# Four samples in rows 0 to 31 and four in rows 32 to 63: the state product of a gated delta layer, split by rows

## The chip, the cores and the metric

The kernel runs on one core of a Trainium2 chip. The metric is device time in microseconds (us) of one execution, the median of several runs.

## What is computed

One step of a hybrid decoder layer, in float32, over 512 prompt tokens and 8 samples of 8 tokens each. What the change touches is the gated delta rule of the sample tokens, with 8 heads of 128 x 128. Cut to that:

```python
def step(s, c):                       # a block of tokens of one sequence and head
    vw_c, kd_c, qk_c, qd_c, ko_c, gl_c = c
    u = vw_c - jnp.einsum('bhcd,bhde->bhce', kd_c, s)
    o = jnp.einsum('bhcd,bhde->bhce', qd_c, s) + jnp.einsum('bhij,bhje->bhie', qk_c, u)
    s = gl_c[..., None, None] * s + jnp.einsum('bhcd,bhce->bhde', ko_c, u)
    return s, o
```

For the samples, b runs over 8 sequences and c over 8 tokens, and `s` is returned as `new_delta_sample`. Per head and sample, the last product of `step` contracts 8 tokens: keys (8 x 128) times `u` (8 x 128) give the 128 x 128 update of the state.

## The kernel before

Channels lie on partitions, tokens along the free axis: 576 columns, 512 of the prompt and 64 of the samples. There are two big parts. The first is the mixing part, a loop of phases n = 0 to 8, written out by hand as 32 slots s for each engine. In phase n TensorE streams the input projection of the next head (the function `dense`, line 558: passes of 288 columns, three for each product, since weights and activations are split in a high and a low part), and between those pieces the delta rule of head n - 1 is worked on, head 1 in phase 1 up to head 8 in phase 8. Phases 2 to 7 are a hardware loop. Below, "head n" is phase n. The second part, from 716 us on, is the output projection (line 567) and the feed-forward part (lines 529 and 883), nearly all TensorE.

The sample state lies in `v["ss"]`, 128 partitions by 8 samples x 128 columns. Its update in phase n has these steps, in the order in which they depend on each other:

- Slot 26: ScalarE writes `u` of the samples, 64 rows (8 samples x 8 tokens) by 128 columns. GpSimd then copies it 8 times side by side into `v["um"]` (64 x 1024), times the mask `rowm`, so that block q keeps only the rows of sample q. It posts `um_ready`.
- Slot 29: GpSimd multiplies `v["ss"]` by its decay and posts `ss_decayed`. It waits for `o_ps`, TensorE's last product for the prompt.
- Slot 30, line 778: TensorE multiplies the keys (`v["ko"]`, 64 rows by 128 columns) with `v["um"]`, in two products of 512 columns into PSUM banks 4 and 5, and posts `ss_ps`. A float32 product is two passes for TensorE, each with its own load of weights.
- Slot 30: VectorE (`sample_state`, line 1338 in the profile) adds the two banks to `v["ss"]` and posts `ss_ready`; two taps of a convolution (line 1341) follow on its queue.
- Slot 31: TensorE sums squares (line 577), ScalarE takes a logarithm and an exponential of the sums (lines 1190 and 1192), and VectorE scales the head's output into `o_a` and posts `head_out`.
- Slot 0 of the next phase: ScalarE (line 1125) waits for `head_out`, and normalizes keys and queries; the chain of the next head runs from there. In its slot 7 TensorE transposes at line 684.

In phase 8 the state isn't added in slot 30: VectorE does it later, in the output part. There GpSimd multiplies blocks of `conf` by a gate (`gate_b`) behind its masked copy, and VectorE adds those blocks to `o_a`.

Every engine has its own queue, which is worked off in order, with waits on counting semaphores.

Of the kernel before, what the change touches and what calls it, by code (L numbers as in the profile page):

```python
# [31 lines left out]
P = 128  # L32
# [3 lines left out]
SEQ = 512  # L36
NS, LS = 8, 8
SMP = NS * LS
# [18 lines left out]
LEVELS_S = 3  # L57
# [22 lines left out]

_LAYOUT = [("ident", P), ("ones", P), ("tri", P), ("suf", P), ("tri_s", SMP), ("suf_s", SMP),
           ("eps", 1), ("eps128", 1), ("big", P), ("big_s", SMP), ("lvl", LEVELS * P),
           ("lvl_s", LEVELS_S * SMP), ("strict", P), ("rowm", NS)]
OFF, _o = {}, 0
for _n, _w in _LAYOUT:
    OFF[_n] = (_o, _o + _w)
# [9 lines left out]
def build(nc, x_t, w_all, w_log, log_par, consts, params, taps, halos, s_in,  # L96
          y_out, s_prompt, s_sample, qkv_rows, conf_rows):
    with ExitStack() as ctx:
# [22 lines left out]
        at, v = 0, {}  # L121
# [46 lines left out]
        def con(nm, rows=P):  # L168
            a, b = OFF[nm]
            return cst[0:rows, a:b] if b <= WIDE else masks[0:rows, a - WIDE:b - WIDE]  # L170
# [13 lines left out]
        def job_ps(j2):  # L184
            return ps[:, 2 * j2:2 * j2 + 2, 0:HALF]

        def g(i):
            return ps[:, 4 + i, :]
# [4 lines left out]
        def two(ap):  # L193
            return ap.rearrange("p (a b) -> p a b", a=2)
# [4 lines left out]
        def tile(ap, c):  # L199
            return ap[:, c * P:c * P + P]  # L200

        def sm(ap, rows=SMP):
            return ap[0:rows, SEQ:SEQ + SMP]

        def smw(ap):
            return ap[0:SMP, SEQ:SEQ + P]
# [176 lines left out]
        def xc_squares(k):  # L383
            nm = ("c4", "extq", "extk", "extv", "qc", "kc", "vc", "gext")[k]
            return v[nm][:, 0:TOK]
# [126 lines left out]
        def _(pe):  # L512
            mm = nc.tensor.matmul
# [60 lines left out]
            def ones_sum(dst, src, start=True, stop=True):  # L574

                for h in range(2):
                    r = mm(dst[:, h], con("ones"), src[:, h * HALF:(h + 1) * HALF],  # L577
                           start=start, stop=stop)
                return r
# [44 lines left out]
            def phase(n):  # L624
                gdn, proj = not first(n), not last(n)
                segs = 0
                for s in range(32):
# [59 lines left out]
                    if s in range(8, 21, 2):  # L687
# [7 lines left out]
                        for c in range(TILES):  # L695
                            r = mm(tile(g(0), c), tile(w, c), tile(t, c),  # L696
                                   start=True, stop=True)
                        if l <= LEVELS_S:
                            r = mm(g(2)[0:SMP, 0:SMP], c_s[(l - 1) % 2][0:SMP], sm(v["dm"]), start=True, stop=True)
                        r.then_inc(x_ps, 1)  # L700
                    if s in range(9, 22, 2):
# [7 lines left out]
                        if l <= LEVELS:  # L709
                            for c in range(TILES):  # L710
                                r = mm(tile(g(0), c), tile(u_r, c), tile(x_r, c), start=True, stop=True)  # L711
                            if l < LEVELS_S:
                                r = mm(g(2)[0:SMP, 0:SMP], v["us"][0:SMP], sm(v["db"]), start=True, stop=True)
                            r.then_inc(dt_ps, 1)
                        for c in range(TILES):
                            r = mm(tile(g(1), c), tile(x_r, c), tile(u_r, c), start=True, stop=True)  # L716
                        if l <= LEVELS_S:
                            r = mm(g(3)[0:SMP, 0:SMP], sm(v["db"]), v["us"][0:SMP], start=True, stop=True)
# [20 lines left out]
                    if s in (22, 24, 26, 28):  # L739

                        c = (s - 22) // 2
                        if c:
                            pe.wait_ge(s_ready, TILES * n - 4 + c)
                        r = mm(g(1)[:, 0:P], tile(u_all, c), tile(v["vt"], c), start=True,  # L744
                               stop=c == 0)
                        if c:
                            r = mm(g(1)[:, 0:P], tile(v["kn"], c), v["s"], start=False, stop=True)
# [3 lines left out]
                    if s in (23, 25, 27, 29):  # L751

                        c = (s - 23) // 2
# [6 lines left out]
                        r = mm(tile(g(3), c), tile(v["u"], c), tile(v["qk"], c), start=c == 0, stop=True)  # L760
                        if c == TILES - 1:
                            r.then_inc(o_ps, 1)
                    if s == 23:
# [5 lines left out]
                        for q in range(NS):  # L769
                            r = mm(two(g(2)[:, 0:2 * SMP])[:, :, q * LS:(q + 1) * LS], tile(v["ss"], q),  # L770
                                   kq[:, :, SEQ + q * LS:SEQ + (q + 1) * LS], start=q == 0, stop=q == NS - 1,
                                   skip_group_check=True)
                        r.then_inc(sz_ps, 1)
                    if s == 30:
                        pe.wait_ge(um_ready, n)
                        pe.wait_ge(s_ready, TILES * n)
                        for q in range(2):
                            r = mm(g(q), smw(v["ko"]), v["um"][0:SMP, q * SEQ:(q + 1) * SEQ],  # L778
                                   start=True, stop=True)
                        r.then_inc(ss_ps, 1)  # L780
                    if s == (30 if last(n) else 31):
# [7 lines left out]
                    if last(n) and s == 20:  # L789

                        pe.wait_ge(xc_ready, KB)
                        for k in range(0, KB, 2):
                            pe.wait_ge(xc_pair, k // 2 + 1)
                            r = ones_sum(job_ps(1), xc_squares(k), k == 0, k == KB - 2)
                        r.then_inc(var_ps, 1)

            phase(0)
            phase(1)
            with pe.Fori(2, H) as n:
                phase(n)  # L800
# [1007 lines left out]
        def _(pool):  # L1808
            gp = nc.gpsimd

            def tt(out, a, b, op):
                return gp.tensor_tensor(out, a, b, op)  # L1812
# [39 lines left out]
            def phase(n):  # L1852
# [8 lines left out]
                for s in range(33):  # L1861
# [97 lines left out]
                        tt(pr(v["um"]), pr(t_r.bitcast(F32)), bc(con("ident")), ALU.subtract).then_inc(tmi_ready, 1)  # L1959
                    if s == 26:  # L1960
                        pool.wait_ge(us_ready, n)
                        tt(v["um"][0:SMP, :].rearrange("p (q c) -> p q c", q=NS),
                           smw(v["u"]).unsqueeze(1).to_broadcast([SMP, NS, P]),
                           con("rowm", SMP).unsqueeze(2).to_broadcast([SMP, NS, P]),
                           ALU.mult).then_inc(um_ready, 1)
                    if s == 29 and not last(n):

# [9 lines left out]
                    if last(n) and s == 31:  # L1977
                        gate_b(7, 0)

            phase(0)  # L1980
            phase(1)
            with pool.Fori(2, H) as n:
                phase(n)
# [45 lines left out]
def shape_constants():  # L2029

    i, j = np.indices((P, P))
    a, b = np.indices((SMP, SMP))
    same = a // LS == b // LS
    out = np.zeros((P, CONSTS), np.float32)

    def put(nm, value, at=0):
        o = OFF[nm][0] + at
        out[:value.shape[0], o:o + value.shape[1]] = value

    def half(r, c, n):  # L2040
        return (r // (2 * n) == c // (2 * n)) & (r // n < c // n)

    put("ident", i == j)
    put("ones", np.ones((P, P)))
    put("tri", i <= j)
    put("suf", i > j)
    put("big", np.where(j < i, BIG, 0))
    put("tri_s", same & (a <= b))
    put("suf_s", same & (a > b))
    put("big_s", np.where(same & (b >= a), 0, BIG))  # L2050
    for l in range(LEVELS):
        put("lvl", half(i, j, 2 ** l), l * P)
    for l in range(LEVELS_S):
        put("lvl_s", half(a, b, 2 ** l), l * SMP)
    put("strict", i < j)
    put("rowm", np.arange(SMP)[:, None] // LS == np.arange(NS)[None, :])
    put("eps", np.full((P, 1), EPS))
    put("eps128", np.full((P, 1), P * EPS))
    return out
# [84 lines left out]
```

## Time and profile before

| | us |
|---|---|
| median of 3 runs | 1191.23 |
| lowest and highest run | 1190.07, 1191.61 |
| the profiled execution | 1191.59 |
| its span, first to last instruction | 1189.5 |

| engine | busy us | share of the span |
|---|---|---|
| TensorE, multiplies | 1148.7 | 97% |
| TensorE, weight loads | 1096.0 | 92% |
| VectorE | 726.2 | 61% |
| GpSimd | 610.2 | 51% |
| ScalarE | 518.5 | 44% |

In the profile's rows PE is TensorE, PEld its weight loads, DVE VectorE, ACT ScalarE, POOL GpSimd and SP SyncE. A row names the line of the kernel, what it writes `<-` what it reads, and the shape; most tiles of the delta rule are parts of one tensor, `work`, and all are called so. The multiplies of TensorE overlap, so that their durations add up to more than the time they take: the distance between two starts is what one costs. GpSimd's tensor operations all have line 1812, VectorE's 1338 or 1341, since a helper issues them; shapes tell them apart.

### The profile page before, as it was taken

To read this page: it belongs to the slowest core of one execution; us is meant where nothing else is said; L and a number is where in the kernel's file an instruction comes from. 1 tells how busy PE (TensorE), PEld (TensorE's weight loads), DVE (VectorE), ACT (ScalarE), POOL (GpSimd) and SP (SyncE) were. 2 spreads that over 40 slices of the span, in tenths; PEclk is the share of its full clock that TensorE was granted. 3 is DMA by queue.
4 is the path that set the end of the run, shared out by engine and by line. 5 is a ranking of instruction groups with operands and counts; after the bars stand their busy time and mean duration, and the time that the engine had idled before them with its cause. 6 is when DMAs were issued, how large, how long until landed. Compare 5 with 4: busy or idle time off the path is not lost.

```text
span 1189.5 us, 22147 instructions
## 1 busy us (share of the span) xinstructions
PE 1148.7 (97%) x8349; PEld 1096.0 (92%) x8349; DVE 726.2 (61%) x1064; ACT 518.5 (44%) x898; POOL 610.2 (51%) x480
## 2 busy tenths in 40 slices
PE   6789999999999999999999989999999999999996
PEld 5689989899899998999989979999999999999996
DVE  6678896886868868778683546764135215314735
ACT  6554545544445354553462576542133123213531
POOL 0338558386584764847657374332433433435841
PEclk9899999999999999999999999999999999999998
DMA  6211223112222122121321116212222222222212
GB/s 236 61 57 45 75 73 100 57 35 81 74 72 83 31 85 74 50 78 44 98 93 41 49 38 222 71 54 72 77 83 90 73 87 88 71 88 89 91 35 80
DMA packets 32519, 92.28 MB, mean 78 GB/s; under 512 B 4688, under 2 KB 12240, under 8 KB 32464
## 3 DMA queue, kind: packets, MB, share of 16 engines
q1 hardware_dynamic: 32464, 91.52, 23.7%
q8 instruction: 38, 0.62, 0.2%
q14 instruction: 17, 0.14, 0.0%
HBM read 82.99 MB, written 8.52 MB: 77 GB/s over the span
## 4 chain that ended last, share of the span: by engine, by line
PE 77%; DVE 11%; issue 6%; ACT 4%; POOL 1%; DMA 0%; DVEq 0%; SPq 0%; ACTq 0%; POOLq 0%
PE ps L529 29%; PE ps L558 23%; PE ps L567 6%; DVE work L1338 5%; PE ps L883 4%; DVE ps L1341 4%; PE ps L716 2%; PE ps L696 2%; PE ps L711 2%; PE ps L770 1%; PE ps L778 1%; PE ps L744 1%; PE ps L577 1%; PE ps L590 1%; DVE o_a L1341 1%
## 5 line engine op out<-in xcount | busy, mean ns | idle before, releaser
L1812 POOL TENSOR_TENSOR w_lo<-raw,w_hi 128x1024 fp32r<-128x1024 f32 x123 | 298.6, 2429 | 380.3 <-ACT w_hi L981 225.8
L558 PE MATMUL ps<-in_hi,w_hi 128*128 128x288 f32 x992 | 305.7, 308 | 3.0 <-ACT work L1058 2.8
L558 PE MATMUL ps<-in_hi,w_lo 128*128 128x288 f32 x992 | 300.3, 303 | 0.0
L558 PE MATMUL ps<-in_lo,w_hi 128*128 128x288 f32 x992 | 299.0, 301 | 0.0
L558 PEld LDWEIGHTS ps<-in_hi,w_hi 128*128 128x128 f32 x992 | 188.9, 190 | 6.6 <-ACT w_hi L963 3.0
L558 PEld LDWEIGHTS ps<-in_hi,w_lo 128*128 128x128 f32 x992 | 188.9, 190 | 2.0
L558 PEld LDWEIGHTS ps<-in_lo,w_hi 128*128 128x128 f32 x992 | 188.8, 190 | 1.2
L1341 DVE SCALAR_TENSOR_TENSOR ps<-work,ct,ps 128x512 f32<-128x512 f32 x240 | 180.7, 753 | 7.4 <-DVE work L1460 1.7
L981 ACT CAST w_hi<-raw 128x1024 fp32r<-128x1024 f32 x61 | 63.8, 1047 | 224.3 <-PE ps L529 224.3
L1338 DVE TENSOR_TENSOR f_tmp<-f_tmp 128x576 f32<-128x576 f32 x31 | 70.7, 2282 | 96.4 <-ACT f_tmp L1288 91.0
L1338 DVE TENSOR_TENSOR o_a<-o_a,ps 128x576 f32<-128x576 f32 (+1 forms) x40 | 25.3, 634 | 144.7 <-PE ps L529 122.8
L529 PE MATMUL ps<-in_hi,w_hi 128*128 128x288 f32 x464 | 99.4, 296 | 0.1
L529 PE MATMUL ps<-in_hi,w_lo 128*128 128x288 f32 x464 | 99.4, 296 | 0.0
L529 PE MATMUL ps<-in_lo,w_hi 128*128 128x288 f32 x464 | 99.3, 296 | 0.0
L963 ACT CAST w_hi<-raw 128x1024 fp32r<-128x1024 f32 x64 | 66.9, 1045 | 36.1 <-PE ps L558 35.1
L529 PE MATMUL ps<-f_lo,w_hi 128*128 128x288 f32 x384 | 82.6, 296 | 0.0
L529 PE MATMUL ps<-f_hi,w_hi 128*128 128x288 f32 x384 | 82.5, 296 | 0.0
L529 PE MATMUL ps<-f_hi,w_lo 128*128 128x288 f32 x384 | 82.5, 296 | 0.0
L1145 ACT ACTIVATE x_r<-ps 128x512 fp32r<-128x512 f32 x48 | 28.8, 599 | 110.7 <-PE ps L696 57.0
L529 PEld LDWEIGHTS ps<-in_hi,w_hi 128*128 128x128 f32 x464 | 74.7, 189 | 0.3 <-issue 0.3
L529 PEld LDWEIGHTS ps<-in_hi,w_lo 128*128 128x128 f32 x464 | 74.8, 189 | 0.0
L529 PEld LDWEIGHTS ps<-in_lo,w_hi 128*128 128x128 f32 x464 | 74.8, 189 | 0.0
(290 smaller groups left out, 2396.0 us busy)
## 6 DMA issues: line engine op xcount, KB each, us to landing
raw<-w_all_in SPq DMA_DIRECT2D x136, 512.0 KB, 3.6
work<-s_in_in SPq DMA_DIRECT2D x8, 512.0 KB, 3.6
s_sample_out<-work SPq DMA_DIRECT2D x8, 512.0 KB, 2.7
xt<-x_t_in SPq DMA_DIRECT2D x4, 576.0 KB, 6.4
xt<-x_t_in SPq DMA_DIRECT2D x2, 1152.0 KB, 7.5
y_out<-o_a SPq DMA_DIRECT2D x16, 144.0 KB, 1.7
halo<-halos_in SPq DMA_DIRECT2D x9, 156.0 KB, 3.4
conf_rows_out<-c_rows SPq DMA_DIRECT2D x8, 135.0 KB, 2.2
```

The lines of the kernel that those rows point to most:

```text
L529: r = mm(ps[:, 2 * w + h, 0:HALF], a[:, k], b[:, k, h * HALF:(h + 1) * HALF], start=k == 0 and p3 == 0, stop=k == KB - 1 and p3 == 2)
L558: t = mm(dense_ps(n, j, h), a[:, w, k], b[:, k, h * HALF:(h + 1) * HALF], start=r == 0, stop=r == PASS_MM // 2 - 1)
L567: r = mm(dst, a[:, k], half_of(b[:, k], h), start=k == 0 and p3 == 0, stop=k == KB - 1 and p3 == 2)
L696: r = mm(tile(g(0), c), tile(w, c), tile(t, c), start=True, stop=True)
L711: r = mm(tile(g(0), c), tile(u_r, c), tile(x_r, c), start=True, stop=True)
L883: r = mm(half_ps(i % 4), a[:, k], half_of(b[:, k], h), start=k == 0 and p3 == 0, stop=k == KB - 1 and p3 == 2)
L963: nc.scalar.copy(w_hi[:, w_buf(n, j)], raw[:, raw_slot(n, j)]).then_inc(w_high, 1)
L981: nc.scalar.copy(weight(m, off)[0], raw[:, (off + 2) % RING]).then_inc(w_high, 1)
L1145: r = A(x_r[:], g(0), ACT.Copy)
L1338: return ve.tensor_tensor(out, a, b, op)
L1341: return ve.scalar_tensor_tensor(out=out, in0=a, scalar=s_, in1=b, op0=op0, op1=op1)
L1812: return gp.tensor_tensor(out, a, b, op)
```

## The change

The keys and the masked `u` contract over 32 rows in each of the two products in place of 64. Product q takes rows 32q to 32q + 31 of both, that is samples 4q to 4q + 3. The masked copy has 4 blocks of 128 columns in place of 8: in rows 0 to 31 block c is sample c, in rows 32 to 63 it is sample 4 + c. The mask has 4 columns. Both products read the same 512 columns of `v["um"]`, from different rows. Results, banks, semaphores, waits and the order on every engine stay as they are.

```diff
@@ -80,7 +80,7 @@
-           ("lvl_s", LEVELS_S * SMP), ("strict", P), ("rowm", NS)]
+           ("lvl_s", LEVELS_S * SMP), ("strict", P), ("rowm", NS // 2)]
@@ -775,7 +775,8 @@
                         for q in range(2):
-                            r = mm(g(q), smw(v["ko"]), v["um"][0:SMP, q * SEQ:(q + 1) * SEQ],
+                            rows = slice(q * SMP // 2, (q + 1) * SMP // 2)
+                            r = mm(g(q), v["ko"][rows, SEQ:SEQ + P], v["um"][rows, 0:SEQ],
                                    start=True, stop=True)
                         r.then_inc(ss_ps, 1)
@@ -1959,9 +1960,9 @@
                         pool.wait_ge(us_ready, n)
-                        tt(v["um"][0:SMP, :].rearrange("p (q c) -> p q c", q=NS),
-                           smw(v["u"]).unsqueeze(1).to_broadcast([SMP, NS, P]),
-                           con("rowm", SMP).unsqueeze(2).to_broadcast([SMP, NS, P]),
+                        tt(v["um"][0:SMP, 0:SEQ].rearrange("p (q c) -> p q c", q=NS // 2),
+                           smw(v["u"]).unsqueeze(1).to_broadcast([SMP, NS // 2, P]),
+                           con("rowm", SMP).unsqueeze(2).to_broadcast([SMP, NS // 2, P]),
                            ALU.mult).then_inc(um_ready, 1)
@@ -2053,7 +2054,7 @@
-    put("rowm", np.arange(SMP)[:, None] // LS == np.arange(NS)[None, :])
+    put("rowm", np.arange(SMP)[:, None] // LS % (NS // 2) == np.arange(NS // 2)[None, :])
```

## Rows read from the trace of the kernel before

**Rows 1.** The page, busy us of each engine (share of the span) and instructions.
```profile
PE 1148.7 (97%) x8349; PEld 1096.0 (92%) x8349; DVE 726.2 (61%) x1064; ACT 518.5 (44%) x898; POOL 610.2 (51%) x480
```
**Rows 2.** The page, shares of the span in the chain that ended last.
```profile
PE ps L529 29%; PE ps L558 23%; PE ps L567 6%; DVE work L1338 5%; PE ps L883 4%; DVE ps L1341 4%; PE ps L716 2%; PE ps L696 2%; PE ps L711 2%; PE ps L770 1%; PE ps L778 1%; PE ps L744 1%; PE ps L577 1%; PE ps L590 1%; DVE o_a L1341 1%
```
**Rows 3.** A stretch: its length, then busy PE, PEld, DVE, ACT, POOL, clock, DMA.
```profile
474.00:550.00 76.00, 75.57 (x552) 70.25 (x552) 58.85 (x94) 36.43 (x72) 48.41 (x48) 1.00 0.21 67
```
**Rows 4.** Line 778: ns min/median/max, first and last start; who waited (us, times).
```profile
L778 PE MATMUL ps<-work x32: 589/589/693, 145.0 to 709.1; 64*128 64x512 f32 x32
...
  DVE work L1338: 9.2, 6
```
**Rows 5.** The chain that ended last, around head 6: start us, us, what.
```profile
526.84 1.92 PE ps L778 x4
...
532.35 0.83 DVE o_a L1341
...
551.77 0.66 PE ps L684 x4
```
**Rows 6.** Timeline of line 778 in head 6: start us, us, engine, line [idle before].
```profile
526.76 0.29 PEld L778 LDWEIGHTS ps<-work 64*128 64x128 f32 x2 [0.17 <-issue]
526.77 0.69 PE L778 MATMUL ps<-work 64*128 64x512 f32 x1
...
527.73 1.02 PE L778 MATMUL ps<-work 64*128 64x512 f32 x2
...
528.16 0.59 PE L778 MATMUL ps<-work 64*128 64x512 f32 x1
```
**Rows 7.** Timeline of head 6, the engines around line 778.
```profile
520.58 1.89 POOL L1812 TENSOR_TENSOR work<-work,masks 64x1024 f32<-64x1024 f32 x1 [0.74 <-ACT work L1172]
...
525.71 3.27 POOL L1812 TENSOR_TENSOR work<-work 128x1024 f32<-128x1024 f32 x2 [3.24 <-PE ps L760]
...
528.78 1.22 DVE L1338 TENSOR_TENSOR work<-work,ps 128x1024 f32<-128x1024 f32 x1 [1.53 <-PE ps L778]
...
529.95 0.74 ACT L1190 ACTIVATE work<-ps,cst 128x576 f32<-128x576 f32 x1 [0.67 <-PE ps L577]
...
531.56 0.76 DVE L1338 TENSOR_TENSOR work<-o_a,work 128x576 f32<-128x576 f32 x1
```
**Rows 8.** TensorE's waits from 474 to 550 us: us in total, times, longest.
```profile
PE ps L684 <- DVE work L1338: 0.4, 1, 0.4
```
**Rows 9.** Timeline of head 1 at line 778.
```profile
144.48 3.12 DVE L1341 SCALAR_TENSOR_TENSOR ps<-work,ct,ps 128x512 f32<-128x512 f32 x4
...
144.99 1.98 PE L778 MATMUL ps<-work 64*128 64x512 f32 x4
...
147.52 1.21 DVE L1338 TENSOR_TENSOR work<-work,ps 128x1024 f32<-128x1024 f32 x1
```
**Rows 10.** GpSimd's groups by shape: count, busy us, mean ns, idle before.
```profile
L1812 POOL TENSOR_TENSOR work<-work,masks 64x1024 f32<-64x1024 f32 x8 | 15.1, 1887 | 5.1 <-ACT work L1172 5.1
...
L1812 POOL TENSOR_TENSOR work<-work 128x1024 f32<-128x1024 f32 x7 | 13.4, 1913 | 22.7 <-PE ps L760 22.7
...
L1812 POOL TENSOR_TENSOR work<-work,masks 128x512 f32<-128x512 f32 x8 | 9.8, 1231 | 0.0
...
L1812 POOL TENSOR_TENSOR work<-cst,hc 128x512 f32<-128x512 f32 x8 | 8.3, 1040 | 43.8 <-DVE hc L1617 43.8
```
**Rows 11.** Timeline of the last head: GpSimd, VectorE, TensorE.
```profile
704.25 7.84 POOL L1812 TENSOR_TENSOR conf<-conf,gate 128x576 f32<-128x576 f32 x5
...
711.35 1.35 DVE L1338 TENSOR_TENSOR conf<-conf,o_a 128x576 f32<-128x576 f32 x1
...
712.63 0.75 DVE L1338 TENSOR_TENSOR conf<-conf,o_a 128x576 f32<-128x576 f32 x1
...
716.32 0.53 PE L567 MATMUL ps<-in_hi,w_more 128*128 128x288 f32 x2 [0.98 <-DVE in_lo L1338]
```
**Rows 12.** The chain that ended last, in the last head.
```profile
706.13 5.82 DVE conf L1338 x4
```

## Prediction, made before the changed kernel ran

> **What bounds the kernel now.** I read the busy shares first. TensorE is busy 97% of the span, VectorE 61%, GpSimd 51% [rows 1], and of a stretch of 76 us, about one head, TensorE is busy 75.57 us [rows 3]. So time taken from TensorE can count, and time taken from GpSimd is suspect until a wait on it is found. The chain that ended last comes next: it gives line 778, the two products that this change rewrites, 1% of the span [rows 2]. The view of that line says why: its 32 passes take 0.59 us each, and VectorE waited 9.2 us for them, six times [rows 4], 1.53 us a time. Six, not eight: heads 2 to 7. In the chain of such a head the four passes (1.92 us) hand over to VectorE, then to `o_a` and ScalarE, and the chain comes back to TensorE only at line 684, 23 us later [rows 5], where TensorE waits 0.4 us [rows 8]. That return is the point to watch: a gain on TensorE alone would become a longer wait at line 684, while a gain that also moves VectorE's step is kept.
>
> **What the change does to TensorE.** There are still two products per head, each 512 columns wide and each in two passes, so 32 passes in all. Nothing shorter is streamed. A pass starts 0.43 us after the one before (527.73 to 528.16) and lasts 0.59 us by its record [rows 6]. What changes is that product 0 uses rows 0 to 31 and product 1 rows 32 to 63, with results in two different PSUM banks. Before, all four passes used rows 0 to 63, one after another. The trace of before shows no pass that starts in a row other than 0, so whether two such passes run side by side has to be bounded. From below: they don't, and four slots stay four (gain 0). From above: product 1 lies wholly beside product 0, and four slots become two (gain 2 x 0.43 = 0.86 us). I take one slot, 0.43 us. TensorE's starts in every timeline stand in program order, and the two passes of a product use the same rows, so the order is 0a, 0b, 1a, 1b: only 0b and 1a are neighbours with different rows. Three slots, then, with the last pass starting at 527.73 and not 528.16.
>
> The Trainium skill, TensorEngine Tiling (Array Packing), Key Properties, says that different tiles can load weights and multiply in parallel, and TensorE: Matmul & The Clock Gate, Part 3, adds that multiplies stay strictly in program order. By these two the gain is the one slot that I took. The same page says that a product over 32 rows alone takes as long as one over 128 rows, so without concurrency it would be nothing. No row here shows concurrency either way.
>
> Where products of 128 rows give way to line 778's of 64, there is a gap of 0.17 us, and the first pass lasts 0.69 us and not 0.59 [rows 6]. That change of shape stays, so it costs nothing new. From row 0 to row 32 the shape stays the same; I take 0 there, with 0.17 + 0.10 = 0.27 us as the other bound.
>
> **Who moves with it, heads 2 to 7.** VectorE's addition starts at 528.78, after a wait of 1.53 us on line 778. It waits also for GpSimd's decay of the states, which starts at 525.71 and takes 1.91 us, to 527.62 [rows 7, 10], and VectorE itself was free at 528.78 - 1.53 = 527.25. So the addition can move forward by up to 1.16 us, and 0.43 fits. ScalarE's logarithm waits 0.67 us for TensorE's sums behind line 778 [rows 7], so it moves 0.43 too, and the next VectorE product at 531.56 needs both. TensorE's own queue is 0.43 us earlier as well. All three arrive at line 684 earlier by the same amount: the wait of 0.4 us stays as it is, and the head is 0.43 us shorter. Six heads: 6 x 0.43 = 2.58 us.
>
> **Head 1: nothing.** There VectorE runs four convolution taps from 144.48 for 3.12 us, to 147.60, and the addition follows at 147.52 without a wait, while TensorE's passes ended at 146.97 [rows 9]. TensorE's 0.43 us turns into a longer wait in the next head.
>
> **What the change does to GpSimd.** The masked copy shrinks from 64x1024 (1.887 us) to 64x512. The nearest rows are the same operation with a mask at 128x512 (1.231 us) and one with a column operand at 128x512 (1.040 us); halving the old one gives 0.94 us [rows 10]. I take 1.2 us, since the operation with a mask has the same kinds of operands: 0.69 us saved, bounds 0.65 and 0.95. In heads 2 to 7 it is worth nothing: the copy starts at 520.58, ends at 522.47, and TensorE comes for it at 526.77 [rows 6, 7]; a cover of 4.3 us.
>
> **The last head: GpSimd's saving counts.** Behind the copy GpSimd has five multiplications of `conf` without a break, 704.25 to 712.09 [rows 11], and VectorE's additions of the same blocks are the chain from 706.13 [rows 12]. A VectorE addition of 128x576 takes 0.75 us alone but 1.35 us where it still overlaps GpSimd [rows 11]. If GpSimd's run ends 0.69 us earlier, at 711.40, the addition at 711.35 is alone nearly from its start and takes 0.75 to 0.8 us. TensorE waits 0.98 us at 716.32 for what follows from it [rows 11], so 0.5 to 0.6 us comes through: 0.57 us (bounds 0.3 and 0.6). Line 778 itself is not on the chain here.
>
> **The small rest.** The constant `rowm` has 4 columns in place of 8, so a load and a cast at the start carry 4 columns fewer of 1416: under 0.01 us. Order and waits of every engine stay the same.
>
> **Sum.** 2.58 + 0.57 = 3.15 us. The profiled execution took 1191.59 us (span 1189.5), so 1188.44 by its own time. The median of the runs is 0.36 us below the profiled one, so I forecast 1188.1 us, 0.26% faster.
>
> **Rivals.**
>
> *No side by side.* Rows 0 to 31 and rows 32 to 63 take turns, and four slots remain. For it: no row shows two passes of line 778 less than 0.43 us apart. Against it: nothing in the trace could have shown it, since all start at row 0. Then only the last head gains: 1191.23 - 0.57 = 1190.7, no change. If the change of rows also cost a gap of 0.27 us, it would be 6 x 0.27 - 0.57 = +1.05, 1192.3, still no change. Chance 0.24.
>
> *Two slots.* Both products run whole beside each other, 0.86 us a head on TensorE. ScalarE then limits: its logarithm can come only 0.67 us earlier [rows 7]. So 6 x 0.67 + 0.57 = 4.6 us, 1186.6. Against it: pass 0b would have to wait behind nothing, though it uses the same rows as 0a. Chance 0.08.
>
> The Trainium skill, TensorE: Matmul & The Clock Gate, Part 3, gives a measured speedup of 3.07 for four products over 32 rows each. [...]
>
> *Slower: loads exposed.* Today the second pass's weights are loaded while the first runs (two loads from 526.76, done at 527.05). A pass that had to wait for the end of the one before, as the first one does with its 0.69 us, would take 0.69 and not 0.43 us of TensorE's time, 0.26 us more [rows 6]. If smaller row groups lost that hiding, three of the four passes would each cost 0.26 us, 0.78 us a head on the chain, since VectorE already waits there: 6 x 0.78 - 0.57 = +4.1 us, 1195.3. It makes the kernel measurably slower from two such passes a head (6 x 0.52 - 0.57 = +2.6). Against it: the 64-row products already hide their second load. Chance 0.08.
>
> **How the numbers follow.** The forecast has a chance of 0.60, with a range of its own from 1187.3 to 1188.9 (the bounds of the last head, 0.3 us, and half of the 1.54 us over which the runs of before spread). Under 0.2% (2.4 us, so above 1188.85) this kernel's measurement can hardly be told from no change; about 0.52 of the 0.60 lies below that. Faster: 0.52 + 0.08 = 0.60. Same: 0.08 + 0.24 = 0.32. Slower: 0.08. The range reaches to two slots below and to no side by side above: 1186.4 to 1191.0; outside it lie the slower rival and a gap between the rows.
>
> **What the new profile would show.** Right: at the two products the third pass starts within some hundredths of the second, the last about 0.86 us after the first (not 1.29), VectorE's wait for it falls from 1.53 to 1.10 us in six heads, the wait at line 684 stays at 0.4 us, and starts of heads drift apart by 0.43 us a head. GpSimd's copy reads 64x512 at about 1.2 us, and the addition in the last head takes about 0.75 us. Wrong: starts 0.43 us apart as now, or the gain on TensorE found again at line 684. What would break the sum is a VectorE wait that turns from line 778 to GpSimd's decay, or a last head in which VectorE and GpSimd overlap all the same.

## The result, and the profile after

| | us |
|---|---|
| median before, 8 runs | 1191.98 |
| median after, 8 runs | 1185.64 (1184.15 to 1188.24) |
| ratio of the times | 0.9947, 95% interval 0.9934 to 0.9960 |
| profiled execution after, its span | 1188.01, 1185.9 |

The change takes 6.3 us, 0.53%, where 3.15 us were forecast; the time lies below the range. The direction was right, the forecast was half of what came. The range was laid from the median of 1191.23 us, from which the result is 5.6 us away; the median of the eight runs of before is 0.75 us higher. In two more comparisons on other chips the ratio was 0.9945 (0.9932 to 0.9958) and 0.9954 (0.9939 to 0.9968).

The profiled execution happens to be one of the slowest of the eight, so its span is only 3.6 us shorter than that of before. I come back to that at the end of the experiments; the parts of a head can be read from it all the same. First the view of the two products' line (779 after; before in [rows 4]): durations in ns as min/median/max, first and last start, who waited (us in total, times, longest us).

```profile
L779 PE MATMUL ps<-work x32: 587/640/692, 145.3 to 703.7; 32*128 32x512 f32 x32
...
  DVE work L1339: 4.1, 6
```

VectorE still waits six times, but 4.1 us in total and not 9.2. The timeline of head 6 around them, to be laid beside [rows 6] and [rows 7] (start us, us, engine, line, and in brackets the idle time before):

```profile
522.80 3.29 POOL L1813 TENSOR_TENSOR work<-work 128x1024 f32<-128x1024 f32 x2 [4.10 <-PE ps L760]
...
523.85 0.30 PEld L779 LDWEIGHTS ps<-work 32*128 32x128 f32 x4 [0.17 <-issue]
523.86 1.13 PE L779 MATMUL ps<-work 32*128 32x512 f32 x4
...
524.91 1.24 PE L577 MATMUL ps<-work,cst 128*128 128x288 f32 x4
525.03 1.22 DVE L1339 TENSOR_TENSOR work<-work,ps 128x1024 f32<-128x1024 f32 x1 [0.69 <-PE ps L779]
525.68 0.69 ACT L1040 ACTIVATE work<-work 128x576 f32<-128x576 f32 x1
526.27 0.72 ACT L1191 ACTIVATE work<-ps,cst 128x576 f32<-128x576 f32 x1
527.03 0.69 ACT L1193 ACTIVATE work<-work 128x576 f32<-128x576 f32 x1
...
527.86 0.76 DVE L1339 TENSOR_TENSOR work<-o_a,work 128x576 f32<-128x576 f32 x1 [0.15 <-ACT work L1193]
```

All four loads now run within 0.30 us, and all four passes within 1.13 us in place of 1.98. Cut to shorter stretches of the same timeline, the four passes fall into two pairs:

```profile
523.86 0.70 PE L779 MATMUL ps<-work 32*128 32x512 f32 x2
...
524.39 0.59 PE L779 MATMUL ps<-work 32*128 32x512 f32 x2
```

In the records a pair's two starts are 6 to 7 ns apart (523.855 and 523.862, 524.389 and 524.395). Two slots, then, not three. The next products, line 577, start 1.06 us after line 779's first pass (524.912 - 523.855); before it was 1.91 us. TensorE gives 0.85 us in each head.

VectorE's scaling of the head's output, at 527.86, comes 4.00 us after the first pass (before, 531.56 - 526.77 = 4.79, so 0.79 us less), and waits 0.15 us for ScalarE, whose three operations from 525.68 on stand one behind the other without a gap. A head is 75.50 us long: the line starts at 448.36, 523.86 and 599.36, where before it started 76.30 us apart. From head 1 to head 2 it is 76.57 us (before 76.58): head 1 gives nothing. The wait at line 684 (before in [rows 8]) is nearly as it was:

```profile
PE ps L684 <- DVE work L1339: 3.0, 6, 0.5
```

This is of the whole run (us in total, times, longest us); before, the same row was 3.0 us in 7 waits. In head 6 alone it went from 0.42 to 0.48 us, of which more below. GpSimd's copy, 1.89 us in [rows 7], takes 1.03 us:

```profile
517.67 1.03 POOL L1813 TENSOR_TENSOR work<-work,masks 64x512 f32<-64x512 f32 x1 [0.73 <-ACT work L1173]
```

### The profile page after: what moved, and what is told of

It reads as the page before. It is cut to its first block, busy times and chain, and to the rows that moved or that the text cites. A ratio compares the mean times of both kernels' runs of the same rounds, so it can differ in the third digit from the quotient of the medians.

```text
span 1185.9 us, 22147 instructions
## 1 busy us (share of the span) xinstructions
PE 1143.2 (96%) x8349; PEld 1093.7 (92%) x8349; DVE 727.3 (61%) x1064; ACT 517.3 (44%) x898; POOL 602.5 (51%) x480
## 4 chain that ended last, share of the span: by engine, by line
PE 78%; DVE 10%; ACT 5%; issue 5%; POOL 1%; DMA 0%; DVEq 0%; SPq 0%; ACTq 0%; POOLq 0%
PE ps L529 29%; PE ps L558 24%; PE ps L567 6%; PE ps L884 4%; DVE work L1339 4%; DVE ps L1342 3%; PE ps L716 2%; PE ps L696 2%; PE ps L711 2%; PE ps L770 1%; PE ps L744 1%; PE ps L577 1%; DVE conf L1339 1%; DVE o_a L1342 1%; PE ps L590 1%
## 5 line engine op out<-in xcount | busy, mean ns | idle before, releaser
L558 PEld LDWEIGHTS ps<-in_hi,w_lo 128*128 128x128 f32 x992 | 189.5, 191 | 2.1
L1339 DVE TENSOR_TENSOR t_r<-t_r,ps 128x512 fp32r<-128x512 f32 x48 | 33.0, 688 | 68.8 <-PE ps L711 61.6
```

What stands on the lines that cost most here:

```text
L558: t = mm(dense_ps(n, j, h), a[:, w, k], b[:, k, h * HALF:(h + 1) * HALF], start=r == 0, stop=r == PASS_MM // 2 - 1)
L1339: return ve.tensor_tensor(out, a, b, op)
```

## The experiments

The theory after the result (A): what a head gains comes from passes over different rows running side by side, in pairs, and GpSimd's copy counts only in the last head. Against it stood that the copy is worth more (B), that the clock's scatter made the gain (C), and that a product over 32 rows is simply faster (D).

### The whole change again, and each half alone

e1 and e9 are the changed kernel itself. e1 to e4 ran beside the kernel before on one chip, e5 to e8 on a second and e9 to e12 on a third; e5, e6 and e7 were run once each, for their traces.

> The changed kernel once more, beside its two halves on the same chip. Theory A (the saving is the four passes of line 779 taking two slots of 0.43 us and not four, 0.80 us in each of heads 2 to 7): starts of line 779 are 75.50 us apart in heads 2 to 7, against 76.30, four passes within 1.13 us, and the time is 4.8 us or a little more below the kernel before. Rival C (a good part of the measured 6.3 us was scatter of the granted clock between runs): the same head period, with times that spread by 3 us or more and follow the granted clock of each run.

The rows alone (e2, e10); GpSimd's copy stays 64x1024:

```diff
-   r = mm(g(q), smw(v["ko"]), v["um"][0:SMP, q * SEQ:(q + 1) * SEQ],
+   rows = slice(q * SMP // 2, (q + 1) * SMP // 2)
+   r = mm(g(q), v["ko"][rows, SEQ:SEQ + P], v["um"][rows, q * SEQ:(q + 1) * SEQ],
```

> TensorE's half alone: the products use rows 0 to 31 and rows 32 to 63, but GpSimd still writes the full 64x1024 masked copy, and product q reads its columns 512q to 512q + 511. Theory A: head period 75.50 us, as with the whole change, and the time within 1 us of it. Rival B (GpSimd's shorter copy is what counts in the time, by way of the last head): the gain falls by 1.5 us or more against the whole change.

The copy alone (e3, e11), against the changed kernel. Both products read the same 512 columns over all 64 rows, so the samples are not kept apart:

```diff
-   r = mm(g(q), v["ko"][rows, SEQ:SEQ + P], v["um"][rows, 0:SEQ],
+   r = mm(g(q), smw(v["ko"]), v["um"][0:SMP, 0:SEQ],
```

> GpSimd's half alone: the masked copy is 64x512, and both products still contract over 64 rows, each over the same 512 columns, so that samples are mixed in the state sums and the sample states are not those of the reference. Theory A: head period 76.30 us as before, four passes 0.43 us apart, time between the one before and 0.6 us below it. Rival B: 1.5 us or more below the kernel before.

| kernel | median us (before, same chip) | ratio, interval | head period |
|---|---|---|---|
| e1 whole | 1186.05 (1192.31) | 0.9945, 0.9932 to 0.9958 | 75.49 |
| e2 rows | 1188.24 (1192.31) | 0.9960, 0.9946 to 0.9974 | 75.49 |
| e3 copy | 1190.75 (1192.31) | 0.9989, 0.9980 to 0.9997 | 76.30 |
| e9 whole | 1185.84 (1191.52) | 0.9954, 0.9939 to 0.9968 | 75.50 |
| e10 rows | 1188.96 (1191.52) | 0.9972, 0.9962 to 0.9983 | 75.48 |
| e11 copy | 1191.45 (1191.52) | 0.9999, 0.9990 to 1.0008 | 76.30 |

VectorE's wait for the products in e3, by the view of their line (us in total, times); in e2 it is 4.1 us, as in the whole change:

```profile
  DVE work L1338: 9.2, 6
```

The head period is decided by the rows alone, to 0.02 us, and the copy moves no head: on that point B falls. The times do not settle what the copy is worth. Alone it takes 1.3 us by the ratio in e3 (1.6 us between the medians) and 0.1 us in e11. Beside the rows it looks larger: e2 is 1.8 us slower than e1 by the ratios (2.2 us between the medians), where A allowed 1 us and B asked for 1.5 us, and e10 is 2.1 us slower than e9 (3.1 us between the medians), where 0.7 us had been expected. The rows alone gave 4.8 us in e2 and 3.3 us in e10. So by their times the halves of the second comparison add up to 3.4 us, and the whole change took 5.5 us. Like stretches of the traces give the copy 0.7 us, as the last section of the experiments shows; the rest of the difference is not explained. The expectations of the second comparison:

> The changed kernel, on one chip with its two halves and with the early square, to see the sum of its parts in the times. By the sections of the traces so far: 4.84 us from the row split (five periods of 0.80 and 0.82 in the seventh), 0.70 us from the shorter copy: 5.5 us below the kernel before, ratio 0.9954. If the scatter of the granted clock falls differently, between 4.5 and 7 us.

> The row split with the full copy once more: 4.8 us below the kernel before and 0.7 us above the whole change. From head 8's state product to the first product of line 529: 78.4 us, against 77.7 with the shorter copy, where one window of low clock falls between 690 and 705 us in both.

> The shorter copy alone once more (samples mixed in the state sums, as before): 0.7 us below the kernel before; if it is 1.5 us or more again, the copy is worth more than the section of the last head shows.

### Is it the separate rows?

e4: both products over rows 0 to 31, so samples 4 to 7 get the sums of samples 0 to 3.

```diff
-   rows = slice(q * SMP // 2, (q + 1) * SMP // 2)
+   rows = slice(0, SMP // 2)
```

> Both products contract over rows 0 to 31 (samples 4 to 7 get the sums of samples 0 to 3, so the sample states are not those of the reference); all else as in the changed kernel. Theory A (passes on different rows run side by side, those on the same rows take turns): four starts 0.43 us apart, as before the change, and a head period of 76.30 us. Rival D (a product over 32 rows is itself faster, or its two passes go side by side whatever the rows): two slots here too, 1.13 us for the four passes and 75.50 us a head.

e6: product 0 over rows 0 to 63, product 1 over rows 64 to 127, with whatever lies there; the sample states are not the right ones here either.

```diff
-   rows = slice(q * SMP // 2, (q + 1) * SMP // 2)
-   r = mm(g(q), v["ko"][rows, SEQ:SEQ + P], v["um"][rows, 0:SEQ],
+   rows = slice(q * SMP, (q + 1) * SMP)
+   r = mm(g(q), v["ko"][rows, 0:P], v["um"][rows, 0:SEQ],
```

> Row groups of 64 in place of 32: product 0 contracts over rows 0 to 63 and product 1 over rows 64 to 127, taking keys of prompt tokens and what lies in the masked copy's columns there (so the sample states are not those of the reference). Theory A (it is the separate rows that count, not that there are 32): two slots, 1.13 us for four passes, head period 75.50 us. Rival D (only products over 32 rows go side by side): four slots and 76.30 us.

The timeline of head 6 in e4:

```profile
527.04 1.98 PE L779 MATMUL ps<-work 32*128 32x512 f32 x4
```

And the same in e6:

```profile
524.09 1.13 PE L779 MATMUL ps<-work 64*128 64x512 f32 x4
```

Over the same 32 rows the four passes take the 1.98 us of before, the head 76.29 us, and VectorE waits its 9.2 us again; over two separate groups of 64 rows they take 1.13 us and the head 75.50 us. So rival D falls: 32 rows are not faster than 64, and it is the separate rows that pair. The whole time of e4, 1191.24 us (ratio 0.9992, 0.9982 to 1.0002), is again that of before. In all these runs the two products write to two different PSUM banks; in e4 that alone made no pair, and whether passes on separate rows would pair within one bank was not tried.

### How do two products make two slots?

My forecast let only neighbours in program order pair. e5 puts a product in between:

```diff
-   for q in range(2):
+   for q in (0, 0, 1):
```

> The changed kernel with product 0 issued twice: rows 0 to 31, rows 0 to 31 again (the same result once more), rows 32 to 63. It asks how passes find their place. Theory A1 (each group of rows works off its own passes, and one that waits does not hold up another group's): six passes in four slots, those of the last product at 0.01 and 0.53 us beside those of the first, the other four 0.43 us apart. Theory A2 (a product goes beside the one just ahead of it in the program and no further): four slots too, but the last product's passes begin with the second product's, at about 0.96 us. Theory A3 (strictly in order of passes, the step that my forecast rested on): five slots. The head period is 76.3 us in A1 and A2, 76.7 in A3.

The timeline of head 6, in four stretches:

```profile
527.19 0.70 PE L779 MATMUL ps<-work 32*128 32x512 f32 x2
...
527.72 1.02 PE L779 MATMUL ps<-work 32*128 32x512 f32 x3
...
528.15 1.02 PE L779 MATMUL ps<-work 32*128 32x512 f32 x2
```

The six passes start at 527.19 (two, 13 ns apart), 527.72 (two, again 13 ns apart), 528.15 and 528.58: four slots, the pairs first. The head period is 76.29 us, 0.79 us more than with two slots. That is A1. Which record belongs to which product can be told by the signal: only the last product of the program posts it, and the record that carries it is the one that starts at 527.735, second of its pair. So the last product does not wait behind the second, whose rows are busy. Each group of rows works off its own passes in these traces; my order 0a, 0b, 1a, 1b was the order of the program and not of the array. What still comes in order is the end: VectorE's addition, which waits for the last product's signal, started only at 529.22, when the last of all passes ended (528.58 + 0.59 = 529.17):

```profile
529.22 1.22 DVE L1339 TENSOR_TENSOR work<-work,ps 128x1024 f32<-128x1024 f32 x1 [1.55 <-PE ps L779]
```

The Trainium skill, TensorE: Matmul & The Clock Gate, Part 3, says that multiplies keep the program's order in start and end. For the signal this case agrees; for the starts e5 does not, since passes of the product between start 0.95 us (528.151 to 527.202) and 0.85 us after those of the product behind it.

### What holds a head at 0.80 us?

TensorE gave 0.85 us and the head 0.80; what lies between them is the longer wait at line 684. In e7 ScalarE's square of the keys (line 1040) moves from behind the table load to slot 29:

```diff
 if s == 29:
+    if not last(n):
+        square_k(n)
     act.wait_ge(o_ps, n)
@@ slot 31
     log_exp()
-    square_k(n)
```

> The changed kernel with one move on ScalarE: the square of the keys goes from behind the table load at line 954 to slot 29, where ScalarE idles 1.4 us, so that the logarithm of line 1191 is no longer behind it. Theory E (ScalarE's queue is what holds the gain of a head at 0.80 us where TensorE gave 0.86): head period 75.43 to 75.46 us. Rival F (another engine holds it): 75.50 us.

> The version with ScalarE's square of the keys in slot 29, timed: head period 75.44 us, six times 0.06 us and so 0.4 us below the changed kernel, less than the scatter of the runs; the trace's period decides, the time only if it is 1 us or more away.

The period is 75.44 us in both runs of this kernel, so theory E holds: ScalarE's queue took the last 0.06 us. Its logarithm now waits for TensorE again (head 6 of e7):

```profile
525.21 1.28 ACT L954 ACT_TABLE_LOAD   x1
527.01 0.74 ACT L1192 ACTIVATE work<-ps,cst 128x576 f32<-128x576 f32 x1 [0.51 <-PE ps L577]
```

TensorE's wait at line 684 is back at its old length. Head 6 of before, of the first profile after, and of e7:

```profile
551.77 0.66 PE L684 MATMUL ps<-cst,c_r 128*128 128x128 f32 x4 [0.42 <-DVE work L1338]
```

```profile
548.07 0.66 PE L684 MATMUL ps<-cst,c_r 128*128 128x128 f32 x4 [0.48 <-DVE work L1339]
```

```profile
548.83 0.66 PE L684 MATMUL ps<-cst,c_r 128*128 128x128 f32 x4 [0.43 <-DVE work L1340]
```

The median of e12 was 1184.20 us (ratio 0.9948, 0.9931 to 0.9964) beside 1185.84 of e9. It is the lowest median of all versions, but the 1.6 us between the two (0.7 us by the ratios) are inside the intervals; the traces carry 0.3 us of them (453.79 against 454.07 us from head 1's product to head 7's).

e8 went further and put the sums (line 577) ahead of the state products on TensorE, and two of VectorE's convolution taps from slot 30 to slot 29:

```diff
@@ TensorE, slot 30
+    pe.wait_ge(o_sq, n)
+    pe.wait_ge(o_read, 2 * n)
+    ones_sum(g2(2), v["gk"]).then_inc(o_sums, 1)
     (the two state products)
-    the same three lines, slot 31
@@ VectorE
-   late = {..., 28: 2, 29: 2, 30: 2, 31: 2}
+   late = {..., 28: 2, 29: 4, 31: 2}
```

> A further version: the square of the keys early as in the run before, TensorE sums the squares (line 577) ahead of the state products, and VectorE takes the two taps of slot 30 in slot 29. The scaling of the head's output then can start at 0.6 us earlier within the head. Theory E (the chain through VectorE and ScalarE ends last, until TensorE's own 0.4 to 0.5 us of waiting at line 684 is used up): head period 75.0 to 75.1 us, 2.4 to 3.0 us less in six heads. Rival G (TensorE's queue ends last already): 75.4 us or more.

The period is 75.57 us, longer than that of e7 (the time: 1186.92 us, ratio 0.9960, 0.9944 to 0.9975). The chain of head 6 shows why (start us, us, what):

```profile
524.51 1.20 PE ps L558 x9
525.72 0.07 issue
525.78 1.21 PE ps L577 x4
526.99 1.06 PE ps L783 x4
528.05 1.78 PE ps L558 x12
529.83 1.94 PE ps L577 x8
531.77 3.44 PE ps L558 x26
...
539.02 0.38 PE ps L663 x2
...
549.94 0.66 PE ps L684 x4
```

By their starts the sums and the products take 2.20 us of TensorE there (525.78 to 527.98). In the changed kernel the products take 1.06 us to the start of line 577, and the sums 0.86 us more to the next one, 1.92 us. TensorE alone is the chain from 518 to 539 us, as rival G had it; from there to line 684 it is mostly VectorE, as in the changed kernel. So the earlier scaling moved nothing behind 539 us, where VectorE waits for TensorE's line 663. Over one head TensorE is busy 75.24 us and not 75.02, and waits 0.07 us ahead of the sums; the wait at line 684 gives back 0.21 us (0.48 to 0.27), and does not go to nothing as theory E had hoped. e8 makes three moves at once, and which of them cost what was not taken apart.

### The last part of the mixing, and the scatter

The stretch from head 7's state product to the first product of line 529 holds the seventh head's gain, the last head and the output projection. TensorE's granted clock from 630 to 645 us sorts the runs (starts from the timelines):

| kernel | from, to | us | clock, 630 to 645 us |
|---|---|---|---|
| before | 603.05, 786.15 | 183.10 | 0.89 |
| e3 copy | 604.81, 787.19 | 182.38 | 0.89 |
| e2 rows | 601.70, 783.96 | 182.26 | 0.89 |
| e4 same rows (copy alone) | 603.33, 784.21 | 180.88 | 1.00 |
| e10 rows | 600.68, 781.61 | 180.93 | 1.00 |
| e1 whole | 599.26, 779.32 | 180.06 | 1.00 |
| first profile after | 599.36, 782.57 | 183.21 | 0.77 |

The row of that stretch in before (stretch, length, busy PE, PEld, DVE, ACT, POOL, clock, DMA share, GB/s):

```profile
630.00:645.00 15.00, 14.03 (x94) 13.00 (x92) 3.53 (x7) 3.75 (x9) 14.33 (x14) 0.89 0.17 46
```

The same in the first profile after:

```profile
630.00:645.00 15.00, 14.03 (x84) 13.18 (x82) 3.12 (x7) 3.08 (x8) 10.87 (x10) 0.77 0.22 70
```

And in e1:

```profile
630.00:645.00 15.00, 14.03 (x107) 13.27 (x106) 3.52 (x8) 4.84 (x10) 13.04 (x12) 1.00 0.23 72
```

Like against like: at 0.89 the copy takes 0.72 us (183.10 to 182.38) and the rows 0.84 us; at 1.00 the rows take 0.82 us (180.88 to 180.06). The copy's 0.87 us at 1.00 (180.93 to 180.06) is less alike, since from 690 to 705 us e10's clock is 0.77 and e1's 0.89. Between 0.89 and 1.00 with the same kernel work lie 1.50 us (e3 to e4), and between 0.77 and 1.00 3.15 us (first profile to e1). In e6, which has the same passes and copy and a clock of 1.00 in all of 630 to 720 us, the stretch takes 180.25 us, 2.96 less than in the first profile.

What the shorter copy does in the last head shows in e3, to be laid beside [rows 11]:

```profile
705.13 7.33 POOL L1812 TENSOR_TENSOR conf<-conf,gate 128x576 f32<-128x576 f32 x5
...
707.79 6.62 DVE L1338 TENSOR_TENSOR conf<-conf,o_a 128x576 f32<-128x576 f32 x5
```

VectorE's five additions start 1.70 us ahead of the state product (707.75 us before, 709.49 in e3) in both, but GpSimd's run beside them ends 1.37 us earlier against it (2.97 and not 4.34 us after it), and they take 6.62 us in place of 7.33. TensorE's wait of 0.98 us in [rows 11] is 0.32 us in e3.

TensorE's busy time from 630 to 645 us is 14.03 us in all three rows above, with a wait of about 1 us in each, and yet its clock was at the lower of its two levels, 1.2 GHz, for part of the stretch in before, for twice that in the first profile after, and never in e1. The runs of one kernel (the first profile after, and e1) differ in it as much as different kernels do. This is why the spans of the first two profiles differ by 3.6 us where the medians differ by 6.3: in the stretch of the table the first profile after gains nothing. There is a second place of scatter. Up to head 1's product the traces of all kernels take from 144.67 to 148.07 us: 144.99 before, 145.28, 145.23 and 144.67 with the whole change, 147.66 and 146.69 with the rows alone, 146.74 and 147.27 with the copy alone. The change does nearly nothing there, and whether the halves are slower there by chance, two traces of each cannot say; it would go some way towards the times of e2 and e10. Rival C is right on the scatter and wrong on the cause: the periods of heads carry the gain.

e9, not in the table, took 181.73 us at 1.00, 1.48 more than e6: its low clock came from 705 to 720 us (0.89), where the output projection starts. Between, from 690 to 705 us, low clock did not add up in the same way: e1, at 0.89 there, took 0.19 us less than e6. From head 7's product to head 8's it took 102.33 us and not 100.83, and got that back behind it, 77.73 and not 79.42 us. VectorE's additions of `conf` are stretched by GpSimd beside them. The timeline of the last head in the first profile after, whose clock is 1.00 from 690 to 705 us:

```profile
700.36 6.82 POOL L1813 TENSOR_TENSOR conf<-conf,gate 128x576 f32<-128x576 f32 x5
...
701.47 8.33 DVE L1339 TENSOR_TENSOR conf<-conf,o_a 128x576 f32<-128x576 f32 x5
```

And in e1, whose clock is 0.89 from 690 to 705 us:

```profile
697.26 7.34 POOL L1813 TENSOR_TENSOR conf<-conf,gate 128x576 f32<-128x576 f32 x5
...
699.89 6.66 DVE L1339 TENSOR_TENSOR conf<-conf,o_a 128x576 f32<-128x576 f32 x5
```

In the first, VectorE starts 1.1 us behind GpSimd and takes 8.33 us; in the second it starts 2.6 us behind, and takes 6.66. The sums end 2.6 us after GpSimd in one and 1.95 us in the other: what a late start costs VectorE it gets back from the shorter overlap.

## Why the prediction was off, step by step

**What bounds the kernel: right.** Line 778 was on the chain in heads 2 to 7 and VectorE waited for it; a saving that TensorE and VectorE share came through, with the wait at line 684 0.06 us longer.

**The slot: the step that failed.** I bounded the saving by 0 and 0.86 us and took one slot, 0.43, because "the order is 0a, 0b, 1a, 1b: only 0b and 1a are neighbours with different rows". The premise, that starts keep the program's order, was read from a kernel in which every pass started at row 0 and could not have shown anything else. Measured: 0.85 us (1.91 to 1.06), the upper bound but for 0.01, and e5 shows the order broken. VectorE's wait fell from 1.53 to 0.69 us, not to 1.10. The rival "two slots" was the right one, at a chance of 0.08. It should have had far more: nothing in the trace spoke against it but the order that I took from passes on the same rows.

**The cap by ScalarE: right in kind, too low in size.** I let ScalarE move by its 0.67 us of waiting. Its logarithm moved by 0.77 (3.18 to 2.41 us behind the first pass), since an operation's recorded duration is not its place in the queue: line 1040 is recorded with 0.69 us, but the next started 0.59 us later. The scaling behind it moved by 0.79, the head by 0.80. e7 shows the cap itself. With 0.80 the rival would have read 6 x 0.80 + 0.57 = 5.4 us, 1185.9 us; the range's lower end of 1186.4, which hung on the 0.67, would have come to about 1185.6, at the edge of the result.

**Change of shape from row 0 to row 32: 0, right.** The second product starts 7 ns after the first.

**Head 1: nothing, right** (76.58 and 76.57 us to the next head).

**GpSimd's copy: right in kind, a little small, and partly by luck.** 1.03 us and not 1.2, and in heads 2 to 7 worth nothing. The last head: 0.57 us forecast, 0.72 measured between like runs. I had one addition, the fourth, fall from 1.35 to 0.75 us. In e3 it did, to 0.74; but the third fell too, from 1.95 to 1.34, and the first grew from 1.62 to 2.13, beside a GpSimd that was further ahead of VectorE all along. Those two nearly cancel.

**The sum.** Forecast 2.58 + 0.57 = 3.15 us. The traces give, for heads 2 to 6, 458.06 - 454.08 = 4.0 us from head 1's product to head 7's, 0.8 for the seventh and 0.7 for the copy: 5.5 us. The three timed comparisons gave 6.3, 6.6 and 5.5 us (by their ratios), and 5.5 lies in each interval. What remains above it in two of them was not traced further; the share of low clock in each run and the stretch ahead of head 1 are the candidates. The time missed the forecast by 2.5 us and the gain by 3.2, since the median that I started from was 0.75 us below that of the eight runs.

**My scatter was too narrow.** I took half of the 1.54 us that three runs spread over; the eight runs of the changed kernel span 4.1 us, those at a mean clock of 0.990 or more within 1184.15 to 1185.27, those at 0.988 or less from 1186.02 up.

## What to carry to other kernels

Where a product contracts over half the rows or less, put independent products on separate groups of rows, one after the other, each with its own bank as here: two float32 products of 512 columns paired completely, both passes. A bound that is reached only if an engine may reorder deserves its own chance when the trace cannot show reordering at all. And read a gain from the period of the loop in one trace rather than from the difference of two spans.

## What the runs showed of the hardware

- Two float32 products of 512 columns on separate row groups take 1.06 us to the next product's start, on the same rows 1.91 us (e4, before); with groups of 32 and of 64 rows alike.
- A later product on free rows starts 13 ns after the first, and so 0.95 us ahead of one between them whose rows are busy (e5), while the reader released by its signal starts only after all passes have ended.
- Four weight loads for two row groups ran within 0.30 us; on one group the third and fourth started with the second and third pass, 0.54 and 0.97 us after the first load (before).
- A mean clock of 0.89 and not 1.00 from 630 to 645 us costs 1.5 us, one of 0.77 costs 3.0 (against e6) to 3.15 us (against e1); one of 0.89 from 690 to 705 us, where VectorE and GpSimd share the work, cost nothing over the whole stretch (e1 against e6).
